# A decoder step on one core: rotation table on GpSimd during the projection, one product moved to VectorE, a stage folded into another, and empty rows left out of a scatter

## The reference, cut to what matters

```
u, q, k, v, qi, ki, wi = split((x * (1 + scale1) + shift1) @ w_in)
abr, abi, bbr, bbi = discretise(a_re, a_im, log_dt, b_re, b_im)   # 32 groups, 64 complex states each
h[t]  = ab * h[t-1] + bb @ u[t]                                   # associative scan over t
y[t]  = Re(c @ h[t]) + d * u[t];  y_ssm = glu(gelu(y))
y_att = attention over the top-k keys that an indexer picks
x = LayerNorm(alpha * x + gate1 * (concat(norm(y_ssm), norm(y_att)) @ w_out))
y[n] = sum over 6 of 64 experts of gate * swiglu_expert(h[n]) + shared_expert(h[n])
x = LayerNorm(alpha * x + gate2 * y)
```

## Time and profile before

| | us |
|---|---|
| runs shown | 2419.93, 2425.22, 2427.26 |
| median | 2425.22 |
| the profiled execution | 2425.9 |
| its span in the profile | 2424.1 |
| TensorE busy | 1979.3 (82%) |
| VectorE busy | 907.8 (37%) |
| ScalarE busy | 594.7 (25%) |
| GpSimd busy | 449.4 (19%) |

### The profile page before, as it was taken

The page is one execution under the profiler, slowest core; times in us unless marked ns, Lnnn a source line. Parts: engine busy times, 40 slices in busy tenths (PEclk is TensorE's granted clock), DMA queues, the critical chain, the costliest instruction groups (busy, mean ns, idle before and its releaser), DMA issues. The chain is left out here.

```text
span 2424.1 us, 29646 instructions
## 1 busy us (share of the span) xinstructions
PE 1979.3 (82%) x9088; PEld 1073.9 (44%) x9089; DVE 907.8 (37%) x2006; ACT 594.7 (25%) x1185; POOL 449.4 (19%) x745
## 2 busy tenths in 40 slices
PE   4799934974369768958998978999999999999965
PEld 1466624542147555535775643333433333333322
DVE  6100074849878753316445731111111111111107
ACT  2100001226749742233111101111111111111114
POOL 0000040034401110000532001222222222222210
PEclk8799976886569679978997998999999999999987
DMA  9700020010000015550242168879889888998767
GB/s 365 259 0 1 1 55 3 3 34 27 18 1 1 1 66 220 221 209 26 93 170 98 45 238 304 288 229 331 268 301 334 279 272 302 327 353 300 260 205 282
DMA packets 89761, 411.30 MB, mean 170 GB/s; under 512 B 21482, under 2 KB 28394, under 8 KB 60363
## 3 DMA queue, kind: packets, MB, share of 16 engines
q1 hardware_dynamic: 62594, 296.24, 31.9%
q0 software_dynamic: 25856, 109.60, 16.5%
q10 hardware_dynamic: 1232, 4.46, 0.5%
HBM read 355.41 MB, written 63.95 MB: 173 GB/s over the span
## 5 line engine op out<-in xcount | busy, mean ns | idle before, releaser
L3130 PE MATMUL psum<-wx,hT_x 128*64 128x512 f32 x2208 | 500.3, 606 | 40.2 <-DMA wx<-in_w_e 27.9
L3130 PEld LDWEIGHTS psum<-wx,hT_x 128*64 128x64 f32 x2208 | 185.2, 139 | 354.8 <-issue 354.8
L3056 DVE COPY hT_x<-psum 128x512 f32<-128x512 f32 x69 | 47.7, 692 | 565.5 <-PE psum L3117 565.5
L3172 PE MATMUL psum<-wx,hidT_x 128*64 128x512 f32 x1104 | 252.1, 598 | 1.3 <-ACT hidT_x L3073 1.3
L3073 ACT COPY hidT_x<-psum 128x256 f32<-128x256 f32 x69 | 25.7, 372 | 501.6 <-PE psum L3156 501.6
L2427 PE MATMUL psum<-wx 128*128 128x512 f32 (+1 forms) x288 | 130.9, 615 | 1.4 <-PEq L2105 1.4
L3172 PEld LDWEIGHTS psum<-wx,hidT_x 128*64 128x64 f32 x1104 | 73.1, 136 | 128.0 <-issue 118.2
L3107 DVE TENSOR_SCALAR y_x<-psum,slot_gate 128x512 f32<-128x512 f32 x69 | 51.8, 751 | 194.8 <-PE psum L3172 189.2
L3046 POOL DMA_INDIRECT scr_acc<-y_x,add_idx x69 | 110.6, 1603 | 32.2 <-issue 32.2
L2427 PEld LDWEIGHTS psum<-wx 128*128 128x128 f32 (+1 forms) x288 | 84.5, 296 | 43.4 <-issue 16.7
L3080 ACT ACTIVATE y_x<-psum,slot_gate 128x512 f32<-128x512 f32 x69 | 47.4, 687 | 222.3 <-PE psum L3172 215.9
(11 more groups left out here) (693 smaller groups left out, 3149.8 us busy)
## 6 DMA issues: line engine op xcount, KB each, us to landing
wx<-in_w_e SPq DMA_DIRECT2D x201, 1024.0 KB, 8.9
wa<-in_w_ada SPq DMA_DIRECT2D x8, 3072.0 KB, 14.0
xt<-in_x_prompt SPq DMA_DIRECT2D x16, 512.0 KB, 4.6
f<-scr_acc SPq DMA_DIRECT2D x16, 512.0 KB, 10.5
scr_acc<-zero SPq DMA_DIRECT2D x11, 512.0 KB, 16.0
wx<-in_w_out SPq DMA_DIRECT2D x2, 2048.0 KB, 12.4
scr_x<-x POOLq DMA_DIRECT2D x8, 512.0 KB, 3.1
scr_h<-h POOLq DMA_DIRECT2D x8, 512.0 KB, 3.8
```

The lines of the kernel that those rows point to most:

```text
L3130: mm = pe.matmul(psum[at, 2 + par, :].rearrange("p (j f) -> p j f", j=2), hT[:, par, k, at], w13[:, :, k], start=(k == 0), stop=(k == KD - 1))
L3172: mm = pe.matmul(psum[at, 5 + c, :], hidT[:, k, at], w2[:, k, c * 512:(c + 1) * 512], start=(k == 0), stop=(k == 1))
```

## The change

- The lower half of `rot` (64 of 128 columns, six doublings) is made by GpSimd during the projection, in `rot_low`, a part of the spare buffer behind `krow`. The tables stage copies it into `rot` on VectorE and makes only the last doubling there.
- The products and sums of `ca` go from GpSimd to VectorE, behind `wz` and ahead of `kmat`, as four products, a wait, and two sums.
- The input stage is gone as a stage. Its transposes stand on TensorE between the turning of c and the matmuls for `kmat`; all nine copies are ScalarE's, which first waits until the low half of `rot` has been read and k has been written out (`k_out`). The samples are loaded straight in the order of `us_g` by eight DMAs of pieces of 64 bytes, and these stand on SP behind the loads of b and ahead of the output of k.
- ScalarE's copies of `wT` wait for `wz_made`, those of `toep` for `k_made`.
- In the routing, the number of an empty row becomes `LANES * ACC` + its partition, which lies behind the table `acc`; the accumulating scatter gets a bound and leaves such rows out.

```diff
+        M, H = PAIRS, CH // 2                                    # project_phase
+        rot, rsq = act_t["rot_low"], act_t["rsq"]
+        @block.gpsimd
+        def _(pool):
+            nc.gpsimd.memset(rot[:, 0, :, 0], 1.0)
+            nc.gpsimd.memset(rot[:, 1, :, 0], 0.0)
+            nc.gpsimd.tensor_copy(rsq[:, 0, 0], cf[:, ROW_AT[5]])
+            done(nc.gpsimd.tensor_copy(rsq[:, 0, 1], cf[:, ROW_AT[6]]))
+            n, cur = 1, 0
+            while n < H:
+                tt(hi[:, 0], lo[:, 0], er, ALU.mult)
+                tt(rt[:, 0, :, 0:n], lo[:, 1], ei, ALU.mult)
+                tt(hi[:, 1], lo[:, 0], ei, ALU.mult)
+                done(tt(rt[:, 1, :, 0:n], lo[:, 1], er, ALU.mult))
+                tt(hi[:, 0], hi[:, 0], rt[:, 0, :, 0:n], ALU.subtract)
+                done(tt(hi[:, 1], hi[:, 1], rt[:, 1, :, 0:n], ALU.add))
...
+                n, cur = 2 * n, 1 - cur
 # ssm_tables_phase, SP
+            for at in range(NT):
+                sp.dma_start(us_g[:, :, at], t["us"][NS + at:2 * NS:NT].rearrange("b (g j) -> b g j", j=GCH)
+                             ).then_inc(us_land, 16)
...
-            sp.wait_ge(rows_out, 96)
+            sp.wait_ge(t["k_out"], 32)
+            sp.wait_ge(rows_out, 64)
 # GpSimd
-            pool.wait_ge(cT_made, 1)
-            ptt(s["ca"][:, 0], fwd[0], cc[0], ALU.mult)
...
 # ScalarE
+            act.wait_ge(rot_moved, 1)
+            act.wait_ge(t["k_out"], 32)
+            for q in range(8):
+                act.wait_ge(uc_ps, q + 1)
+                nc.scalar.copy(uc[:, 4 * q:4 * q + 4, 0:CH], ...).then_inc(uc_read, 1)
+            act.wait_ge(uc_ps, 9)
+            nc.scalar.copy(uc[:, :, CH:CHS], ...).then_inc(uc_read, 1)
+            act.wait_ge(wz_made, 1)
...
-            act.wait_ge(ca_chain.sem, 6)
+            act.wait_ge(k_made, 1)
 # VectorE
-            while n < CH:
...
+            nc.vector.tensor_copy(rot[:, :, :, 0:half], low).then_inc(rot_moved, 1)
+            dve.wait_ge(rot_moved, 1)
+            cmul((rot[:, 0, :, half:], rot[:, 1, :, half:], rot[:, 0, :, 0:half], rot[:, 1, :, 0:half], er, ei,
+                  rt[:, 0, :, 0:half], rt[:, 1, :, 0:half]))
...
+            nc.vector.tensor_tensor(s["ca"][:, 0], fwd[0], cc[0], ALU.mult)
+            nc.vector.tensor_tensor(s["ca"][:, 1], fwd[0], cc[1], ALU.mult)
+            nc.vector.tensor_tensor(tmp_ca, fwd[1], cc[1], ALU.mult)
+            seq(nc.vector.tensor_tensor(tmp2, fwd[1], cc[0], ALU.mult))
+            nc.vector.tensor_tensor(s["ca"][:, 0], s["ca"][:, 0], tmp_ca, ALU.add)
+            seq(nc.vector.tensor_tensor(s["ca"][:, 1], s["ca"][:, 1], tmp2, ALU.subtract))
             dve.wait_ge(k_ps, 1)
 # TensorE
+            for q in range(8):
+                if q >= 4:
+                    pe.wait_ge(uc_read, q - 3)
+                for g in range(4):
+                    mm = pe.transpose(psum[:, 4 + q % 4, g * P:(g + 1) * P], ...)
+                mm.then_inc(uc_ps, 1)
+            pe.wait_ge(us_land, 16 * NT)
+            for g in range(GROUPS):
+                mm = pe.transpose(psum[:, 0, g * NB:(g + 1) * NB], us_g[:, g]...)
+            mm.then_inc(uc_ps, 1)
             pe.wait_ge(wz_made, 1)
+            pe.wait_ge(uc_read, 9)
 # route_phase
-            nc.vector.tensor_scalar(empty_at[:], part_f[:], float(TRASH + 1), None, ALU.add)
+            nc.vector.tensor_scalar(empty_at[:], part_f[:], float(LANES * ACC + 1), None, ALU.add)
 # expert_phase
-                    in_=y[:, j % 2], in_offset=None, compute_op=ALU.add).then_inc(added, 16)
+                    in_=y[:, j % 2], in_offset=None,
+                    bounds_check=LANES * ACC - 1, oob_is_err=False, compute_op=ALU.add).then_inc(added, 16)
```

More of the change, by code:

```diff
@@ L347, in project_phase, with done, tt @@
         block = ctx.enter_context(nc.Block())
+        M, H = PAIRS, CH // 2
+        rot, rsq = act_t["rot_low"], act_t["rsq"]
+        rt = sb("rt", [P, 2, M, H // 2])
+        turns = Chain(sem("turn_chain"))
+        @block.gpsimd
+        def _(pool):
+            def done(ins):
+                pool.wait_ge(turns.sem, turns.did(ins))
+            def tt(out, x, y, op):
+                return nc.gpsimd.tensor_tensor(out, x, y, op)
+            nc.gpsimd.memset(rot[:, 0, :, 0], 1.0)
[4 more added lines that the diff above has]
+            while n < H:
+                nar = [P, M, n]
+                er, ei = (rsq[:, cur, i].unsqueeze(2).broadcast_to(nar) for i in range(2))
+                lo, hi = rot[:, :, :, 0:n], rot[:, :, :, n:2 * n]
+                tt(hi[:, 0], lo[:, 0], er, ALU.mult)
[4 more added lines that the diff above has]
+                done(tt(hi[:, 1], hi[:, 1], rt[:, 1, :, 0:n], ALU.add))
+                c, d = rsq[:, cur, 0], rsq[:, cur, 1]
+                new_c, new_d = rsq[:, 1 - cur, 0], rsq[:, 1 - cur, 1]
+                tt(new_c, c, c, ALU.mult)
+                tt(rt[:, 0, :, 0], d, d, ALU.mult)
+                tt(new_d, c, d, ALU.mult)
+                done(tt(rt[:, 1, :, 0], d, c, ALU.mult))
+                tt(new_c, new_c, rt[:, 0, :, 0], ALU.subtract)
+                done(tt(new_d, new_d, rt[:, 1, :, 0], ALU.add))
+                n, cur = 2 * n, 1 - cur
         def evacuate(eng, g):
@@ L616, in ssm_tables_phase @@
         shift = sb("shift", [P, P + (LC - 1) * GCH])
-        rsq = sb("rsq", [P, 2, 2, M])
+        us_g = sb("us_g", [NB, GROUPS, NT, GCH])
+        uc, rsq = s["uc"], t["rsq"]
         rt = free[:, M * P:2 * M * P].rearrange("p (i m c) -> p i m c", i=2, m=M)
@@ L727, in _ @@
             PR, PI, FR, FI, R8, C8, S8 = ROW_AT
[L729 to L734, removed]
-            while n < CH:
[L736 to L745, removed]
+            rot, low, half = s["rot"], t["rot_low"], CH // 2
+            levels = half.bit_length() - 1
+            er, ei = (rsq[:, levels % 2, i].unsqueeze(2).broadcast_to([P, M, half]) for i in range(2))
+            nc.vector.tensor_copy(rot[:, :, :, 0:half], low).then_inc(rot_moved, 1)
+            dve.wait_ge(rot_moved, 1)
+            cmul((rot[:, 0, :, half:], rot[:, 1, :, half:], rot[:, 0, :, 0:half], rot[:, 1, :, 0:half], er, ei,
+                  rt[:, 0, :, 0:half], rt[:, 1, :, 0:half]))
             seq(nc.vector.memset(cb[:], 0.0))
@@ L803, in _ @@
             pe.wait_ge(shift_made, 2)
[L804 to L808, removed]
+            for at in range(LC):
+                if at >= 4:
+                    pe.wait_ge(t_read, at - 3)
+                off = GCH * (LC - 1 - at)
+                mm = pe.matmul(psum[:, at % 4, :], shift[:, off:off + P], kmat[:].rearrange("p g i -> p (g i)"),
```

98 lines of the change are left out of this document (27 added, 71 removed).

## The result

The changed kernel takes 2364.66 us (median of 4 runs, 2363.71 to 2364.76) against 2425.12; the ratio is 0.9754, 95% interval 0.974 to 0.9769. The forecast was 2365. The profiled execution took 2364.76 us, its span is 2363.0: 61.1 less than before. The scan's first load is issued 51.2 us earlier than in the earlier trace rows, and the stretch from the first up matmul (1466.23 before, 1415.99 after) to the end of the span is 947.0 us instead of 957.9; between the two there is 1 us of scatter the other way.

The account below looks back on a forecast made before the run. It took the tables and input stages before the scan, with VectorE late beside GpSimd, and TensorE's waits for expert weights as the bounds; 2425.9 - 50.5 (tables, input) + 0.5 (projection) - 11 (experts) = 2364.9, forecast 2365 us, range 2344 to 2383.

Parts of the forecast that it names:

- Rotations: Tables stage: VectorE keeps one copy and one doubling of the rotation table; TensorE's input ready at 352.9, 35.9 us earlier.
- Why VectorE was late: Tables stage before the change: VectorE takes turns with GpSimd's six ca products of 3.95 us each, and VectorE pays.
- ca: Tables stage: ca on VectorE ends at 366.6, hidden behind TensorE's 13.86 us of small matmuls at the lower clock; costs nothing.
- Rival (d): More gain than counted: upper clock in table matmuls (-5) or most of the experts' 31 us; 2340 to 2353, chance 0.17.
- Input: Input folded into tables stage: k output lands at 340.1 to 342.4, copies ready at 349.0 to 351.3; costs nothing.
- rival (c): Input comes late because the k output lands after 344.0: +1 to +13.5 us, 2366 to 2378; chance 0.10.
- The tail: Tables stage from 352.9: the old 27.1 us, then 0.3 between stages; scan's first load at 380.3, -50.5 us.
- Projection: GpSimd makes the low rotations in 26 us, hidden; VectorE's scaling of h at the front may wait: +0.5, bounds 0 and 4.
- Experts: Scatter skips 26% of rows: -11 us, from 6.3 of weight waits, 3.4 of slow matmul groups, 1 of the last scatter.
- Rival (b): Experts: skipped rows don't bring weights earlier, since the loads queue behind each other; 2376 us, chance 0.20.
- rival (e): Experts: the bounds check makes each scatter longer, so the kernel is slower; 2473 us at 5 us a scatter, chance 0.03.

## Why the prediction was right, step by step

- **Rotations.** Forecast: doubling from 325.7, clearing of c_b from 333.6 with the mask of dmat beside the doubling, TensorE's start at 352.9. Measured: 325.70, 333.67, 353.01.
- **Why VectorE was late.** "Both engines are taking turns, and VectorE pays" is shown by the runs that move one part each: 35.8 us at the start of the table matmuls are some 22 of turns shared with GpSimd and some 13 to 14 of VectorE's own small levels. The six products take 3.85 to 4.64 us each in the kernel before, 25.0 together; I had written 3.95 for each of them.
- **ca.** Forecast 366.6 for its end and a lower clock for TensorE; measured 366.57 and 13.86 us at 0.50. Rival (d)'s part on the clock didn't come by itself, but the runs with unread transposes brought 2.2 to 2.5 of its 4 to 5 us in that stage.
- **Input.** The us loads held SP 6.42 us, not 4.8 (the eight loads of the samples in the old input stage, of another shape, had held it 5.68), so the k output was issued 1.1 us later than I said. ScalarE was released at 341.01, between my 340.1 and 342.4. The second half of the output landed 4.9 us after its issue, as it did with sixteen loads ahead of it, and 4.6 with none (4.8 in the earlier trace rows): the loads cost SP's time and no landing. The Trainium skill, DMA: Bandwidth & Descriptors, section on why a DMA increments its semaphore by 16, says that a transfer whose slowest dimension is eight is served by eight engines; the 2.3 us that I worked out from this for the landing are not in the rows. The copies ended at 348.04, earlier than 349.0, mainly because the last transposes ran for the most part at the upper level (granted clock 0.89, 2.37 us instead of 3.55). (Of the three copies that I counted, 0.42 us is not in the earlier trace rows: in the kernel before it was VectorE's copy, and ScalarE's takes 0.37.) Cost: nothing, as forecast, and rival (c) is out.
- **The tail.** From the table matmuls to the scan's load 26.56 us instead of 27.4 (27.1 and 0.3 between stages). Together the term is -51.2, forecast -50.5.
- **Projection.** I put 0.5 us between 0 and 4; it was 0. GpSimd's front:

```profile
103.43 0.67 POOL L360 TENSOR_TENSOR att<-att,rsq 128x16 f32<-128x16 f32 x1
...
105.50 1.37 POOL L360 TENSOR_TENSOR rt<-att,rsq 128x16 f32<-128x16 f32 x1
...
107.88 0.21 POOL L360 TENSOR_TENSOR rsq<-rsq 128x16 f32<-128x16 f32 x1
```

Here GpSimd pays: its products take 0.67 to 1.37 us while VectorE scales h (until 106.2) and 0.21 afterwards, and VectorE's five take 3.70 us, 3.71 before. Later in the stage VectorE pays as well: its two copies into wq, beside GpSimd's largest products, take 1.78 and 2.06 us instead of 1.22 each, which costs nothing there, since TensorE waits for neither. GpSimd's whole work lasts 31.6 us, to 134.0, where I had 26.

- **Experts.** Forecast -11 as 6.3 of waits, 3.4 of slow groups and 1 of the last scatter. In the pair of profiles it is -10.9: 5.5 of waits, 5.1 of slow groups, nothing from the last scatter (the final stage's first load is issued 9.1 us after the end of GpSimd's last instruction in both, and still 7.5 us after it with every row skipped). As a mean over 13 profiles it is -8.7, so the profiled pair flatters the forecast by 2. The slow groups vary as much: 5.5 with full scatters and 3.4 with 2304 rows skipped on the mean, two spared as forecast, but the changed kernel had three in one profile and five in the other. I had also said that the wait named after the expert weights would fall to near 20 us; it fell from 27.9 to 26.4, and the rest of the 5.5 stands under "issue" (12.3 to 8.3): the sum of the two was the thing to forecast. Rival (b) is refuted by the run with the skipping alone, rival (e) by the scatter's 1602 ns.

That the total fits to 0.3 us is partly luck: the tables gave 0.7 more, the experts some 2 less than in the forecast, and a run's other stretches scatter by more than that.

## What to carry to other kernels

When one engine's tiny instructions last as long as another engine's big ones beside them, the two are taking turns: move the big ones off, or put them where the other engine has nothing to do; the gain here was nearly the length of what was moved (22 to 23 of 25 us), with two different neighbours. A stage that is short on one engine can be folded into the wait of another stage if its inputs are issued early enough, and the margin can be measured by doubling the loads. Fewer scattered rows beside a stream of weight loads paid here in proportion, 3.7 to 3.8 us per thousand rows of 4 KB, but in waits and in slow matmul groups both, so sum them before naming a releaser.

## What the runs showed of the hardware that was not expected

- The 64 small table matmuls, which keep TensorE busy for 15.99 of 16 us, ran at 0.50 throughout when they began at that level. Begun at the upper one, they fell back to 0.50 on the way although TensorE stayed busy: in the run with 40 unread transposes from 1.00 (357 to 361 us) to a mean of 0.63 (361 to 366), and in the run with doubled loads almost at once (1.00 until 352.7, a mean of 0.52 from 353.2 to 360). The level rose under transposes too: the 40 ran at 0.50 to 353 us, then at a mean of 0.69 to 357.
- A skipped row still makes a packet: 19296 on GpSimd's queue with and without, while those under 512 bytes in the expert stretch rise by 2304 (7416 to 9720). GpSimd's wait for a scatter to land hardly falls with 26% of the rows skipped (331.9 to 331.0 us over 68 steps), but it falls to 96.6 us, in 33 waits, with all of them skipped.
- The same 32 transposes of the samples, at the same place, took 2.37 us in one profile (granted clock 0.89) and 3.58 in others (0.50 in the run with 24 unread transposes).
